# Value products of eight sequences in column strips of TensorE, on a hybrid decoder step

## The reference

```python
o_c = jnp.einsum('bgrqn,bngd->bqgrd', p_c.astype(v_c.dtype), v_c)        # compressed, 63 rows
o_s = jnp.einsum('bgrqnk,bgqnkd->bqgrd', p_s.astype(v_g.dtype), v_g)     # selected
o_w = jnp.einsum('bgrqw,bwgd->bqgrd', p_w.astype(v_w.dtype), v_w)        # window
o = gate[..., 0, None] * o_c + gate[..., 1, None] * o_s + gate[..., 2, None] * o_w
```

## Time and profile before

| | us |
|---|---|
| median of 3 runs | 1908.9 |
| the runs | 1902.18, 1908.9, 1911.46 |
| span of the profiled execution, first to last instruction | 1908.5 |
| of it PE busy | 1799.0 (94%) |
| DVE, ACT, POOL busy | 729.2, 390.5, 273.8 |
| mean granted TensorE clock | 0.964 of 2.4 GHz |

### The profile page before, as it was taken

How to read it: one execution, slowest core, us unless ns; L and a number is a source line. 1 busy time by engine, 2 the same in 40 slices (tenths; PEclk the granted TensorE clock), 3 DMA queues, 4 the chain that set the end, 5 groups by cost and what they waited for, 6 DMA issues and landing times.

```text
span 1908.5 us, 25111 instructions
## 1 busy us (share of the span) xinstructions
PE 1799.0 (94%) x9323; PEld 1369.5 (72%) x9323; DVE 729.2 (38%) x1319; ACT 390.5 (20%) x862; POOL 273.8 (14%) x286
## 2 busy tenths in 40 slices
PE   7999999698688999999999899999999999999996
PEld 3464454577265666776776689899899899898894
DVE  2100333222313444665564413533533434434437
ACT  2100211132101233332332311111112112112112
POOL 1210121211200000000000111311211212212212
PEclk9999999698977899999999999999999999999999
DMA  8220100534611000000000121121121111111202
GB/s 288 73 94 0 44 1 6 139 89 127 166 52 54 4 4 4 4 4 1 4 1 0 34 67 34 34 66 33 37 62 33 47 52 33 56 43 33 64 13 89
DMA packets 91320, 94.74 MB, mean 50 GB/s; under 512 B 6352, under 2 KB 74545, under 8 KB 91153
## 3 DMA queue, kind: packets, MB, share of 16 engines
q1 hardware_dynamic: 69410, 73.99, 12.6%
q0 software_dynamic: 4240, 11.32, 2.0%
q10 hardware_dynamic: 17600, 8.47, 1.7%
HBM read 86.61 MB, written 11.34 MB: 51 GB/s over the span
## 4 chain that ended last, share of the span: by engine, by line
PE 86%; DVE 5%; issue 3%; DMA 2%; ACT 1%; SPq 1%; ACTq 1%; POOL 0%; POOLq 0%; DVEq 0%
PE bankpair L338 13%; PE bankpair L1779 9%; PE bankpair L1781 9%; PE bankpair L1780 9%; PE bankpair L1438 7%; PE bankpair L1407 6%; PE bankpair L1806 5%; PE bankpair L1497 5%; PE bankpair L1807 5%; PE bankpair L1808 5%; PE bankpair L819 3%; PE bankpair L1476 2%; PE bankpair L1117 1%; DMA work<-in_state_win_kv 1%; PE bankpair L1394 1%
## 5 line engine op out<-in xcount | busy, mean ns | idle before, releaser
L1779 PE MATMUL bankpair<-h2T_high,w_high 128*128 128x344 f32 x1056 | 337.9, 320 | 0.0
L1781 PE MATMUL bankpair<-h2T_high,w_low 128*128 128x344 f32 x1056 | 337.1, 319 | 0.0
L1780 PE MATMUL bankpair<-h2T_low,w_high 128*128 128x344 f32 x1056 | 337.0, 319 | 0.0
L338 PE MATMUL bankpair<-work 128*128 128x512 f32 (+3 forms) x720 | 288.7, 558 | 0.8 <-DMA work<-in_w_in 0.8
L1909 DVE TENSOR_TENSOR x_all<-x_all,bankpair 128x512 f32<-128x512 f32 (+1 forms) x396 | 251.7, 684 | 1.7
L338 PEld LDWEIGHTS bankpair<-work 128*128 128x128 f32 (+1 forms) x720 | 127.4, 180 | 145.9 <-issue 137.0
L1895 DVE TENSOR_TENSOR kT_space<-kT_space,bankpair 128x344 f32<-128x344 f32 x66 | 33.8, 513 | 451.4 <-ACT kT_space L1843 451.4
L1779 PEld LDWEIGHTS bankpair<-h2T_high,w_high 128*128 128x128 f32 x1056 | 198.6, 188 | 3.1 <-issue 0.2
L1780 PEld LDWEIGHTS bankpair<-h2T_low,w_high 128*128 128x128 f32 x1056 | 198.1, 188 | 1.1 <-issue 0.2
L1781 PEld LDWEIGHTS bankpair<-h2T_high,w_low 128*128 128x128 f32 x1056 | 198.4, 188 | 0.0
L1830 POOL TENSOR_TENSOR w_low<-work,w_high 128x1024 fp32r<-128x1024 f32 x44 | 105.6, 2425 | 565.4 <-ACT w_high L1825 565.4
(11 more groups left out here) (270 smaller groups left out, 2102.5 us busy)
## 6 DMA issues: line engine op xcount, KB each, us to landing
work<-in_w_gate SPq DMA_DIRECT2D x22, 512.0 KB, 5.1
work<-in_w_up SPq DMA_DIRECT2D x22, 512.0 KB, 6.3
work<-in_w_down SPq DMA_DIRECT2D x22, 512.0 KB, 3.8
work<-in_w_in SPq DMA_DIRECT2D x4, 2048.0 KB, 8.1
x_all<-in_x_prompt SPq DMA_DIRECT2D x8, 512.0 KB, 12.5
work<-in_cache_kv_cmp SPq DMA_DIRECT2D x32, 128.0 KB, 2.9
work<-in_cache_kv_cmp POOLq DMA_DIRECT2D x32, 128.0 KB, 2.9
work<-in_cache_kv_slc POOLq DMA_DIRECT2D x32, 128.0 KB, 3.8
```

The source lines that it names most:

```text
L338: ins = pe.matmul(pb(at_n % 4)[0:n, 0:w], hT[:, k, P * t:P * t + n], wslot[c % 2][:, k, 0:w], start=(k == 0), stop=(k == KD - 1))
L1779: pe.matmul(out, wh, high, start=(k == 0), stop=False)
L1780: pe.matmul(out, wh, low, start=False, stop=False)
L1781: ins = pe.matmul(out, wl, high, start=False, stop=(k == KD - 1))
```

## The change

Four sequences form a group. Within a group the matmuls go by kind, and for each kind one after another over the four sequences, each with `tile_position=(0, 32 * (s % 4))`: its 8 stationary columns are loaded into a column strip of 32 of its own, and its output lies on the partitions of that strip, 0 to 7, 32 to 39, 64 to 71 or 96 to 103. The first group writes 128 columns of `pb(2)`, the second of `pb(3)`. The copy to `o_rows` takes all 128 partitions of the two pieces of 128 columns, the partitions between the outputs with it; two turns of 128 x 128 replace eight of 8 x 128, and the copy to `oT_s` picks the 8 columns of each sequence from its 32. The four waits for the streams of a group stand ahead of the group.

```diff
-    o_rows = at(0, [NB, P])
+    NSTRIP = 4
+    o_rows = at(0, [NB // NSTRIP, P])
...
-        for s in range(NB):
-            wait_stream(pe, s)
-            cols = slice(NH * s, NH * s + NH)
-            o = bank[1][0:NH, P * s:P * s + P]
+        def own(s):
+            return slice(NH * s, NH * s + NH)
+
+        def strip(s):
+            return pb(2 + s // NSTRIP)[32 * (s % NSTRIP):32 * (s % NSTRIP) + NH, 0:P]
+
+        for first in range(0, NB, NSTRIP):
+            seqs = range(first, first + NSTRIP)
+            for s in seqs:
+                wait_stream(pe, s)
             for br, col in ((0, 384), (1, 640)):
-                pe.matmul(o, pnT[0:NB, br, cols], kv_new[:, col:col + P], start=(br == 0), stop=False, skip_group_check=True)
-            pe.matmul(o, pcT_s[0:CMP_N, cols], vc_s[0:CMP_N, s, :], start=False, stop=False, skip_group_check=True)
+                for s in seqs:
+                    pe.matmul(strip(s), pnT[0:NB, br, own(s)], kv_new[:, col:col + P], start=(br == 0), stop=False,
+                              tile_position=(0, 32 * (s % NSTRIP)), skip_group_check=True)
+            for s in seqs:
+                pe.matmul(strip(s), pcT_s[0:CMP_N, own(s)], vc_s[0:CMP_N, s, :], start=False, stop=False,
+                          tile_position=(0, 32 * (s % NSTRIP)), skip_group_check=True)
             for c in range(NTILE):
-                pr = pT_slc[:, c, cols] if c < 8 else pT_win[:, c - 8, cols]
-                ins = pe.matmul(o, pr, v_rows[s][:, c, :], start=False, stop=(c == NTILE - 1), skip_group_check=True)
+                for s in seqs:
+                    pr = pT_slc[:, c, own(s)] if c < 8 else pT_win[:, c - 8, own(s)]
+                    ins = pe.matmul(strip(s), pr, v_rows[s][:, c, :], start=False, stop=(c == NTILE - 1),
+                                    tile_position=(0, 32 * (s % NSTRIP)), skip_group_check=True)
             ins.then_inc(seq_valued, 1)
         pe.wait_ge(o_rows_taken, 1)
-        for s in range(NB):
-            ins = pe.transpose(pb(0)[:, NH * s:NH * s + NH], o_rows[0:NH, s, :], ident[0:NH, 0:NH])
+        for n in range(NB // NSTRIP):
+            ins = pe.transpose(pb(0)[:, P * n:P * n + P], o_rows[:, n, :], ident[:, :])
...
-        dve.wait_ge(seq_valued, NB)
-        dve.tensor_copy(o_rows[0:NH].rearrange("p s n -> p (s n)"), bank[1][0:NH, :]).then_inc(o_rows_taken, 1)
+        dve.wait_ge(seq_valued, NB // NSTRIP)
+        dve.tensor_copy(o_rows, bank[1].rearrange("p (n c) -> p n c", n=2)[:, :, 0:P]).then_inc(o_rows_taken, 1)
         dve.wait_ge(o_rows_turned, 1)
-        dve.tensor_copy(oT_s, pb(0)[:, 0:64]).then_inc(oT_taken, 1)
+        dve.tensor_copy(oT_s.rearrange("p (n h) -> p n h", n=NB), pb(0)[:, 0:2 * P].rearrange("p (n c) -> p n c", n=NB)[:, :, 0:NH])\
+           .then_inc(oT_taken, 1)
```

## The result

The changed kernel takes 1884.38 us, the median of four runs (1881.22 to 1885.95), against 1908.38 for the kernel before: a ratio of 0.987 with a 95% interval of 0.9845 to 0.9895, thus 1.05 to 1.55% faster. Measured once more after the experiments, the ratio was again 0.987 (0.9843 to 0.9896). The forecast was 1886.5.

A forecast was written before the change was run, and what follows sets the result against it. It took TensorE's unbroken value products (31.96 us), with nothing beside them, as the bound. Products -21.2, copy -0.8 and turn -0.3 gave -22.3 us, thus 1886.5 us; range 1879 to 1901.

The forecast's parts named there:

- The path: Value products, 31.96 us on TensorE with nothing beside them: a microsecond saved there is a microsecond of the end.
- The products, -21.2 us: Value products: four strips stream at once, so two groups replace eight sequences; -21.4 us, plus 0.2 us for strip offsets.
- The offset of the strips: Value products: starts some 13 ns apart from strip to strip, costing 0.2 us in all.
- Rival B: Value products: strict start order lets only two strips run at a time; -16.0 us, 1892.8 us; chance 0.15.
- The prediction's other estimate for the warm group, 4.5 us: Second group at full clock: 4.5 us instead of 3.56, from the skill page's estimate of 3.2 times for four strips.
- C: Value products: strips run one after another, only form changes, copy and turn save; -2.9 us, 1906 us; chance 0.10.
- D: Value products: each of 120 strip changes costs 0.19 us, making the kernel slower; +19.3 us, 1928 us; chance 0.07.
- Copy and turn, -1.1 us: Behind the products: VectorE's result copy -0.79 us, two turns in place of eight -0.27 us, second copy zero.
- The prediction's gap of 256 columns: VectorE's result copy: the gap between its two pieces is just a second row of the same pattern.
- The clock: TensorE's clock behind the change may fall at other times; expected zero, bound 4 us either way.

The follow-up runs named there:

- the runs above: Changed kernel with two, three, four, six or twelve matmuls in a row per strip in the 128-row part; that part of group two took 2.83 to 9.31 us.
- The run by sequence: Changed kernel with its strips, copy and turn, but all 15 matmuls of one sequence before the next, as in the kernel before; 1907.39 us, ratio 0.998.
- The run in one strip: Changed kernel's interleaved order, but all outputs on partitions 0 to 7, with the copy and turn of the kernel before; 1906.82 us, ratio 1.000.

## Why the prediction was right

By its own steps:

- *The path.* That a microsecond of the stretch is one of the end held: the waits of three engines shrank together, and counted from the first product stage 4's first load came 22.5 us earlier (563.08 - 527.65 = 35.43 us before, 538.17 - 525.21 = 12.96 after), as much as the stretch and its tail lost. In the timeline it stands at 538.17 us and not near 541, because the first product itself began 2.4 us earlier.
- *The products, -21.2 us.* Measured -21.46. The row that carried it was L1127's, a pitch of 26 ns where 53 was due; its starts lie 13, 46, 12, 44, 12, 43 and 13 ns apart, two by two, as the prediction read it. Two row halves ran at once there, and four column strips did here. The pitch came out at 26.7 ns for 27. The offset of the strips was put at 13 ns from strip to strip, 0.2 us for both groups; it was 5 to 8 ns, and the groups took 0.06 and 0.10 us more than a sequence at the same clock (6.82 for 6.76, 3.66 for 3.56). What makes the sum larger than forecast all the same is the clock: the second sequence of before began at the low clock and took 3.81 us, the second group did not.
- *Why L1127 could do it* I had not seen. Its heads 0 to 3 come first and 4 to 7 behind them: four for one half, exactly what a column strip takes by the runs above. If a row half takes no more, which no run tested, a fifth turn on the lower half would have held up the upper one. The changed kernel alternates after two pairs, so it stays within the four with room to spare. The prediction did not ask how far TensorE looks past a busy strip; that its row and its change both lie within that reach was luck.
- *Rival B.* Its premise, pairs starting strictly in program order, is the rule of the Trainium skill's "TensorE: Matmul & The Clock Gate", Part 3, that the prediction weighed. It falls: with four pairs in a row for each strip, strict order would let only the last of a run overlap the first of the next, 24 x 3 + 1 = 73 steps for 96 pairs, and 26.0 were measured. What is in order is the issue; that starts are in order within a strip fits all six lengths. The prediction's other estimate for the warm group, 4.5 us, fell too: it took 3.66.
- *Rivals C and D.* The run in one strip shows what C would have been: 31.72 us, and no gain to be measured. D falls with the pitch; a change of strip costs nothing that shows.
- *Copy and turn, -1.1 us.* Measured -1.01: copy 1.22 to 0.44 us, turn 0.67 to 0.45, second copy 0.23 to 0.24. The run by sequence has both without the products' gain, and its tail is 2.47 us, before 3.47. The turn in two pieces alone was not tried. The prediction's gap of 256 columns between the pieces that are copied is 384 (128 of each bank's 512 are read); it had put no price on it.
- *The clock.* Put at zero with 4 us either way. Inside the stretch it rose and fell nearly as assumed. Outside it, the profiled pair differs by 3.4 us in favour of the change, and stage 4's range of 8.5 us over the kernels is about the width that the bound allowed.
- *The number.* The medians differ by 24.0 us, the profiled pair by 25.9, the changed part by 22.5 and the forecast's sum was 22.3. Wherever the record has both, a time is 1.7 to 2.0 us longer than the span of the same execution (1884.58 and 1882.6 us for the changed kernel). So the execution that was profiled before took about 1910.4 us, an estimate, and was some 2 us slower than the median of 1908.38; that its span lies 0.4 us below a median says nothing. The 1.5 us by which the medians differ more than the changed part are less than the spread of either kernel's runs (1902.18 to 1911.46 and 1881.22 to 1885.95), and no run traces them: that the time lies 2.1 us under the forecast is not explained. Two sums of the prediction are 0.1 us off, its 1886.5 (1886.6) and rival B's 1892.8 (1892.9); nothing hangs on them.

## What to carry to other kernels

Where a stationary operand has few columns (8 here, in strips of 32), four independent accumulations in four column strips take the time of one, but only if the program alternates strips often enough: here every four load-and-matmul pairs at the latest, which is two float32 matmuls. With six in a row half as much again is paid (4.18 us for 2.78), and with 24 little of the gain is left (9.31 us, where one after another takes 10.9). And a change of a few microseconds should be judged by its stretch in the profile: behind it stage 4 alone differs by 8.5 us from one kernel to another, and by 6.9 us between two executions of the same one.

## What the runs showed of the hardware that I had not expected

- Each column strip takes up to four pairs, the running one included, and a fifth stops the program for all strips: 25.5, 26.0, 38.3, 54.0, 69.7 and 85.4 steps for 2 to 24 pairs in a row. In the trace of 24 in a row the last four of a strip run beside the first four of the next. Whether the room is counted in pairs or in something that goes with them at these sizes is open.
- No overlap crossed a change of row form: with whole sequences one after another each took 3.56 us, although the end of one and the start of the next lie in different strips. The next strip's first pair started 0.20 us after the start of the last one there, and 5 or 6 ns after that of the fourth from the end where the row form was the same (24 in a row).
- The clock rose 10.1 us after the first product when the stretch began with 24 pairs of few rows one after another (one strip, four interleaved), and 5.3 to 7.3 us after it in ten other traces. It is one trace, and that its beginning caused this is not shown.
